# Summing the outputs of 64 experts into the tokens: 0/1 products on TensorE in place of a scatter to memory, with the down product moved inside each step

## What is computed

```python
MOE_EXPERTS = 32; MOE_TOP_K = 2; EXPERT_HIDDEN = 512   # D_MODEL 1024, SEQ 512
...
    gp, gi = lax.top_k(group_prob, 1)          # one of 4 groups
...
    ev, ei = lax.top_k(sel, MOE_TOP_K)         # two of its 8 experts
    gates = gp * jax.nn.softmax(ev, axis=-1)
...
        hid = jax.nn.silu(xblk @ w_gate[e]) * (xblk @ w_up[e])
        return hid @ w_down[e]
...
    yr = yb.reshape(n_rows, d).astype(F32) * row_gate[:, None]
    return jax.ops.segment_sum(yr, row_tok, num_segments=n_tok).astype(x2.dtype)
```

## Time and profile before

| | us |
|---|---|
| median of 3 runs | 1770.22 |
| the profiled execution: its own time | 1770.5 |
| its span, from the first to the last instruction | 1768.7 |
| TensorE busy | 1561.2 |
| VectorE busy | 565.6 |
| ScalarE busy | 323.9 |
| GpSimd busy | 133.4 |

### The profile page before, as it was taken

The page is one execution under the profiler, slowest core; times in us unless marked ns, Lnnn a source line. Parts: engine busy times, 40 slices in busy tenths (PEclk is TensorE's granted clock), DMA queues, the critical chain, the costliest instruction groups (busy, mean ns, idle before and its releaser), DMA issues.

```text
span 1768.7 us, 22309 instructions
## 1 busy us (share of the span) xinstructions
PE 1561.2 (88%) x9199; PEld 1003.0 (57%) x9199; DVE 565.6 (32%) x924; ACT 323.9 (18%) x547; POOL 133.4 (8%) x136
## 2 busy tenths in 40 slices
PE   8999998987788777879999999999997878977776
PEld 6876785543344444437777787878653444544342
DVE  4899743110101101125452444454311101101104
ACT  4225630100000000023221222222010000000002
POOL 0030001111011011000000000000110110111010
PEclk9999999999999999999999999999999999999998
DMA  8521157999999999995122122227599999999996
GB/s 290 191 76 68 60 197 273 401 400 392 398 406 407 399 399 406 397 366 193 60 95 96 48 96 95 84 107 304 214 396 404 409 406 409 402 402 404 400 404 254
DMA packets 117930, 495.60 MB, mean 280 GB/s; under 512 B 14153, under 2 KB 26441, under 8 KB 84928
## 3 DMA queue, kind: packets, MB, share of 16 engines
q1 hardware_dynamic: 104576, 467.69, 67.8%
q0 software_dynamic: 10176, 16.24, 2.8%
q10 hardware_dynamic: 3072, 10.18, 1.5%
HBM read 484.66 MB, written 26.74 MB: 289 GB/s over the span
## 4 chain that ended last, share of the span: by engine, by line
PE 46%; SPq 30%; DMA 14%; DVE 6%; issue 2%; ACT 1%; DVEq 0%; ACTq 0%; POOLq 0%
SPq L771 30%; PE psum L833 9%; PE psum L834 8%; PE psum L835 8%; PE psum L917 6%; PE psum L941 3%; DMA in_pair<-in_expert_w_up 3%; DMA in_uT<-in_expert_w_up 3%; DMA raw<-in_expert_w_up 3%; DMA raw<-in_expert_w_gate 3%; PE psum L1287 2%; DVE xs L1701 2%; PE psum L926 2%; PE psum L908 1%; DMA xs_dram<-xs 1%
## 5 line engine op out<-in xcount | busy, mean ns | idle before, releaser
L917 PE MATMUL psum<-raw,xeT 128*64 128x256 f32 x2048 | 247.2, 388 | 79.9 <-DMA raw<-in_expert_w_gate 41.1
L917 PEld LDWEIGHTS psum<-raw,xeT 128*64 128x64 f32 x2048 | 145.1, 138 | 171.7 <-DMA raw<-in_expert_w_up 51.0
L1987 DVE TENSOR_TENSOR hid<-silu_g,psum 128x256 f32<-128x256 f32 (+1 forms) x64 | 27.5, 430 | 650.4 <-PE psum L917 621.7
L917 PE MATMUL psum<-in_pair,xeT 128*64 128x256 f32 x1280 | 155.7, 390 | 49.3 <-DMA in_pair<-in_expert_w_up 33.8
L647 DVE TENSOR_TENSOR w_lo<-raw,w_hi 128x2048 fp32r<-128x2048 f32 x46 | 105.4, 2291 | 202.2 <-ACT w_hi L641 202.2
L917 PEld LDWEIGHTS psum<-in_pair,xeT 128*64 128x64 f32 x1280 | 90.5, 139 | 108.5 <-DMA in_pair<-in_expert_w_up 47.5
L641 ACT ACTIVATE w_hi<-raw 128x2048 fp32r<-128x2048 f32 x46 | 88.0, 1914 | 339.1 <-PE psum L835 335.0
L1496 ACT ACTIVATE y_e<-psum 64x512 f32<-64x512 f32 (+1 forms) x60 | 35.6, 594 | 597.7 <-PE psum L941 575.8
L833 PE MATMUL psum<-w_hi,uT_hi 128*128 128x512 f32 x352 | 139.1, 395 | 1.6 <-DVE h L2130 1.4
L835 PE MATMUL psum<-w_lo,uT_hi 128*128 128x512 f32 x352 | 137.2, 390 | 0.0
L834 PE MATMUL psum<-w_hi,uT_lo 128*128 128x512 f32 x352 | 137.1, 390 | 0.0
(11 more groups left out here) (245 smaller groups left out, 1935.3 us busy)
## 6 DMA issues: line engine op xcount, KB each, us to landing
raw<-in_expert_w_gate SPq DMA_DIRECT2D x88, 1024.0 KB, 24.2
raw<-in_expert_w_up SPq DMA_DIRECT2D x44, 1024.0 KB, 24.6
free_a<-in_expert_w_down SPq DMA_DIRECT2D x44, 1024.0 KB, 24.9
free_b<-in_expert_w_down SPq DMA_DIRECT2D x44, 1024.0 KB, 24.9
in_pair<-in_expert_w_up SPq DMA_DIRECT2D x42, 1024.0 KB, 24.6
in_uT<-in_expert_w_up SPq DMA_DIRECT2D x42, 1024.0 KB, 24.7
in_pair<-in_expert_w_gate SPq DMA_DIRECT2D x40, 1024.0 KB, 24.2
xs<-in_expert_w_down SPq DMA_DIRECT2D x40, 1024.0 KB, 24.9
```

The costliest lines, as they stand in the source:

```text
L917: mm = nc.tensor.matmul(psum[c * FIRST:(c + 1) * FIRST, bank, 0:HID // 2], x[:, j, 0:FIRST], w[:, j, c * HID // 2:(c + 1) * HID // 2], sta ...
```

## The change

What it does:

- All 32 experts are summed by 0/1 products. Each result is scaled by its gate on the way out of PSUM and split into `y_hi` (ScalarE) and `y_lo` (VectorE), both fp32r. In every second step the two finished experts of the pair before are added to the four tiles of tokens: per tile eight products (two experts, high and low, two halves of 512 columns) into PSUM banks 1 and 7, then VectorE adds both banks to `h` (`add_sum`). The 0/1 matrices are made per tile and pair by VectorE (`tokens_of`). The last three experts (29 to 31) are summed at the end (`last_sums`).
- The scatter, `y_dram` in the usual path, the eight loads back, the eight stores of zeros, `gate_early` and `gate_diag` are gone. They stay only for `over_pass`.
- A step on TensorE becomes: gate, turn `hid` of the last step, turn the next tokens, down of the last step, up. The queue of weights follows this order (`BLOCKS`).
- VectorE works out a gate for each slot of each step (`place_gates`) before step 0.
- Tokens are turned at a width of 64 (before: 96), all eight pieces in one bank.

```diff
-EARLY = 3
+EARLY = 4
...
+BLOCKS = ([("gate", 0), ("up", 0)] +
+          [block for e in range(1, STEPS) for block in (("gate", e), ("down", e - 1), ("up", e))] + [("down", STEPS - 1)])
...
+SUM_BANKS = (1, 7)
+SUMS = [(e, e + 1) for e in range(0, BIG, 2)] + [(BIG,)] + [(e, e + 1) for e in range(BIG + 1, STEPS - 3, 2)]
+SUM_IN_STEP = {steps[-1] + 2: n for n, steps in enumerate(SUMS)}
+LAST = tuple(range(SUMS[-1][-1] + 1, STEPS))
...
+                def sum_tile(e, q):
...
+                    pe.wait_ge(m.token_ok, at + 1)
+                    pe.wait_ge(m.y_lo_ok, past + SUMS[n][-1] + 1)
+                    if at:
+                        pe.wait_ge(m.added, at)
...
+                    for i, of in enumerate(SUMS[n]):
+                        for y in (y_hi, y_lo):
+                            for half in range(2):
+                                r = slice(0, P) if of == BIG else slice(half * FIRST, (half + 1) * FIRST)
+                                src = y[half] if of == BIG else y[of % 2][r]
+                                mm = nc.tensor.matmul(psum[:, SUM_BANKS[half]], to_token[r, at % 2, i], src,
+                                                      start=(i == 0 and y is y_hi), stop=(of == SUMS[n][-1] and y is y_lo))
+                    mm.then_inc(m.summed, 1)
...
                 for e in range(STEPS):
                     if e:
-                        turned(e - 1)
+                        pe.wait_ge(m.silu_ok, past + e)
...
+                    w, ready = weights("gate", e)
+                    product(xeT[:, e % 2], w, 2, ready, m.gate_psum)
+                    if e:
+                        turned(layer, e - 1)
+                    sum_tile(e, 0)
...
+                        transpose_tokens(m, x_e[:, (e + 1) % 2], rows_in_step(e + 1))
+                    sum_tile(e, 1)
                     if e:
-                        down(e - 1)
...
+                        down(layer, e - 1, *weights("down", e - 1))
+                    sum_tile(e, 2)
+                    w, ready = weights("up", e)
+                    product(xeT[:, e % 2], w, 3, ready, m.up_psum)
+                    sum_tile(e, 3)
...
+            def add_sum(layer, n, q):
+
+                dve.wait_ge(main.summed, sum_no(layer, n, q) + 1)
+                for half in range(2):
+                    dst = h[:, q, half * 512:(half + 1) * 512]
+                    ins = V.tensor_tensor(dst, dst, psum[:, SUM_BANKS[half]], ALU.add)
+                ins.then_inc(main.added, 1)
...
+                    n = SUM_IN_STEP.get(e)
+                    if n is not None:
+                        add_sum(layer, n, 0)
+                        tokens_of(layer, n, 2)
+                    if e < STEPS - 1:
+                        copy_tokens(m, past + e + 2, xeT[:, (e + 1) % 2], rows_in_step(e + 1))
+                    if n is not None:
+                        add_sum(layer, n, 1)
+                        tokens_of(layer, n, 3)
+                        add_sum(layer, n, 2)
+                    elif e:
+                        keep_y(layer, e - 1)
...
-            def scatter(m, e, b):
-
-                G.indirect_dma_start(y_dram, bass.IndirectOffsetOnAxis(ap=rows_of(e, 1), axis=0), y_e[0:rows_in_step(e), b], None,
-                                     bounds_check=TOPK * SEQ - 1, oob_is_err=False).then_inc(m.scattered[b], 16)
```

More of the change, by code:

```diff
@@ L1074, in over_pass, with last_sums, some @@
                 pe.wait_ge(over_landed[layer], over_total(layer))
-            def sums(layer):
-                def last_rows(q, i, start=False, stop=True, counted=False):
-                    for n, y in enumerate((last_hi[i][:, :], last_lo[:, i])):
+            def last_sums(layer, last_down, spilled):
+                m, past = main, STEPS * layer
+                slot = [e % 2 for e in LAST[:-1]] + [2]
+                def some(q, i):
+                    for n, y in enumerate((y_hi[slot[i]], y_lo[slot[i]])):
                         for half in range(2):
@@ L1087, in last_rows @@
+                            if i == len(LAST) - 1 and n:
                                 mm.then_inc(bank_full[b], 1)
-                def gated_rows(q, half, first=True):
-                    b, _, _ = banks.at("last", layer, q, half)
-                    c = slice(half * 512, (half + 1) * 512)
-                    pe.wait_ge(rows_in[q], 32 * (layer + 1) + 16)
-                    pe.wait_ge(diag_ok, sum(len(tiles) for tiles in BY_PRODUCT[:layer + 1]) * TOPK)
-                    for k in range(TOPK):
-                        mm = nc.tensor.matmul(psum[:, b], gate_diag[:, BY_PRODUCT[layer].index(q) * TOPK + k], y_back[k][q][:, c],
-                                              start=(first and k == 0), stop=(not first and k == TOPK - 1))
-                    return mm
@@ L1100, in sums, with early @@
-                pe.wait_ge(last_lo_ok, 2 * layer + 1)
-                last_rows(0, 0, True, False)
-                pe.wait_ge(last_lo_ok, 2 * layer + 2)
-                for q in range(TILES if layer else TILES - 1):
-                    by_product = q in BY_PRODUCT[layer]
-                    if by_product:
-                        for half in range(2):
-                            gated_rows(q, half)
-                    if q:
-                        last_rows(q, 0, not by_product, False)
-                    last_rows(q, 1, counted=True)
+                def early(q):
+                    for i in range(len(LAST) - 1):
+                        some(q, i)
@@ new lines, in last_sums @@
+                turned(layer, STEPS - 1)
+                if spilled:
+                    down(layer, STEPS - 1, *last_down)
+                    over_pass(layer)
+                pe.wait_ge(m.last_token_ok, layer + 1)
+                pe.wait_ge(m.added, sum_no(layer, len(SUMS) - 1, TILES - 1) + 1)
+                pe.wait_ge(m.y_lo_ok, past + STEPS - 1)
+                early(0)
+                early(3)
+                if not spilled:
+                    down(layer, STEPS - 1, *last_down)
@@ L1111, in sums @@
+                early(1)
+                pe.wait_ge(m.y_lo_ok, past + STEPS)
+                for q in range(TILES):
+                    if q == 2:
+                        early(2)
+                    some(q, len(LAST) - 1)
                 if not layer:
-                    q = TILES - 1
-                    last_rows(q, 0, True, False)
-                    last_rows(q, 1, stop=False)
                     norm_tile(2, 0)
-                    for half in range(2):
-                        b, _, _ = banks.at("last", layer, q, half)
-                        gated_rows(q, half, False).then_inc(bank_full[b], 1)
```

420 lines of the change are left out of this document (204 added, 216 removed).

## The result

The changed kernel takes 1721.09 us (median of 4 runs, 1718.56 to 1725.76) against 1769.43 us (4 runs, 1768.29 to 1770.52): a ratio of 0.9728, interval 0.9714 to 0.9741. It is 48 us faster; 40 were forecast. The profiled execution is the slowest of the four, 1725.76 us, so trace stands against trace with 44.7 us. In a few runs of several kernels, the one before among them, TensorE's granted clock was 0.96 to 0.97 and the time 2% longer; no comparison or range here holds one of these.

The account below looks back on a forecast made before the run. An expert stage was taken to be bound by weight transfers. -16.8 - 4.9 - 13.9 + 0.5 - 4.6 = -39.7 from 1770.5 gave 1731 us; likeliest case (both sides near 472 us, 55%) 1722 to 1742, range 1710 to 1753.

Parts of the forecast that it names:

- The idle spell: Weight queue near the start of each layer's expert stage: blocks asked for in order of use remove 5 us idle.
- The scatter: Transfers in the expert stages: dropping it saves 0.55 us in each of 29 steps, 16 us a layer (10 to 25).
- Transfers 470.8 and 466.4: First gate product to last up product in layers 0 and 1, in us, if transfers alone set the time.
- TensorE, 472: TensorE's own need per layer from first gate to last up product: 395.5 us plus 76.5 us of sums.
- x: TensorE's cost of one group of sums, taken as 5.1 us; the change is 30x - 197 us, no gain at 6.6.
- The additional 3 and 1.5 us for two equal chains: Expert stages of layers 0 and 1: added because TensorE and transfers at times wait for each other.
- Tails: From U, the end of a layer's last up product: -4.9 us to layer 0's second weight split, -4.6 to the last norm.
- Rival 1: Sums on TensorE cost more, x of 6.8 to 8.2, and the kernel is slower: 1777 to 1819 us; 7%.
- Rival 2: Sums cost somewhat more, x of 5.6 to 6.4, and TensorE binds alone: 1742 to 1765 us; 15%.
- Rival 3: Cheap sums, x of 4.4, and a dear scatter, 0.87 us a step: 1705 us, with half of this 1718; 16%.
- Rival 4: Transfers do not shrink without the scatter; only the gains from idle queue and layer ends come: 1751 us; 5%.
- rival 5: Second pass runs or block order leaves the weight queue as idle as before: within 0.2% or slower; 2%.

Follow-up runs that it names:

- the order alone: The kernel before with only the new order of products on TensorE and of blocks in the weight queue, scatter and loads back kept: 1757.56 us.
- the low part twice: The changed kernel with the products of y_lo in the sums issued twice: 1775.53 us, ratio to the kernel before 1.0032.

## Why the prediction held

The forecast was 1731 us, its likeliest range 1722 to 1742, the whole range 1710 to 1753; 1721.1 lies just below the likeliest case's own range. The mechanism held: two nearly equal bounds took the place of one. Of the 10 us that it is off, 5 are the spread of the changed kernel (its profiled run is 4.7 us above its median), 5 are in the terms. That some terms came out so closely is in part luck, as two of them below show.

- **The idle spell, -5 us a layer.** Right in layer 0 (-5.4 by the order alone), half in layer 1 (-2.6), for a reason that stays open.
- **The scatter, -0.55 us a step.** Right where the transfers alone bind: 0.59. Put back beside the full sums it was worth 11.1 and 9.2 us a layer, where 16 and 10 were forecast. Its share was taken as half of 5.3%; it was 2.1 points, 5.5 engine-us a step and 0.35 us if spread evenly. So the step's forecast was right with too large a share and too even a spread: 0.59 is 1.7 times the even 0.35, near the doubling that half of the engines would give, but no view here shows single engines, and the share of 0.46 at 772 us is a mean that doesn't tell how many were done. The Trainium skill (DMA: Bandwidth & Descriptors, The descriptor swizzle) has partitions 0 to 31 on engines 0 to 7 in a transfer to 128 partitions. A factor of 1.7 does not contradict that, but a scatter of 64 slots is not that transfer, and the -25 us that the rule was taken to give was 17.1.
- **Transfers 470.8 and 466.4.** Measured 470.7 and 468.0.
- **TensorE, 472.** Layer 1, where nothing else bound, took 473.4. This is partly luck, for the parts missed in opposite directions: x was 5.3 against 5.1, a step without sums 11.9 (23.78 / 2) against 12.07, and the clock, for which the sum has no term, cost 2.2 and 4.1 us. At the full clock it is 469.3 to 469.5. The first pair of a tile takes 0.34, the others 0.23 to 0.24, as read from the earlier trace rows. The Trainium skill (TensorEngine Tiling (Array Packing), Key Properties) says that a change of mode drains the engine. The 0.1 us that was charged for it, eight times a group, fits the timeline, where the first pair takes from 377.50 to 377.84 us, 0.34 against 0.23.
- **The additional 3 and 1.5 us for two equal chains.** This was the wrong term. In layer 0 the 472.2 are TensorE's 469.5 at the full clock, 2.2 of clock and 0.5 of waiting for the last half block; the one chain hindered the other by that 0.5 us and no more. In layer 1 it did not at all. The missing term for the clock is what makes 473.4 meet the forecast of 473.5.
- **Tails.** -4.7 for -4.6 and, with the 1.5 us at the next block, -5.6 for -4.9. The landing of the next mixer's weights is not what ScalarE waited for: its split starts at U + 10.3, right behind `y_hi`. But the norm starts at U + 15.3, not 13.7. 1.35 us of this is `last_token`, made by VectorE after `hid` only. From U of layer 0 to S of layer 1 the kernels with the new sums take between 469.6 and 471.3 us, so a term under 2 us there, like this 1.5, is not told from the spread by one profile.
- **place_gates, +0.5.** It cost 1.2, inside its bounds of 0 to 1.3.
- **S of layer 0, -1.9.** Not foreseen; the store of rows, which the first gather waited for before (18.7 us, now 16.6), is a wait that the prediction didn't look at.
- **30x - 197, no gain at x = 6.6.** With the low part twice x is 7.2 and the kernel is 0.3% slower than before. By the measured 1721.1 at 5.3 the line crosses zero at 6.9. Rival 1 was thus the right shape at the wrong price: its x of 6.8 would have ended near no change. Rival 2 began at x = 5.6, above the 5.3. It reached up to 1765 us, so the range to 1753 holds only the lower part of it, although the prediction says that it takes it in. Rival 3 asked for a cheap x and a dear scatter, and had neither. Rival 4 fell with the 17.1 us of the scatter, rival 5 with the full queue from S + 8 us on.

## What to carry to other kernels

When a change moves work from the queue that binds to the engine that waits, work out both sides to the microsecond: the gain ends where they meet, and here they met within 2 us in layer 0 and 6 in layer 1. Afterwards a chain of 85% TensorE does not mean that TensorE alone binds; take work away from it and add the same amount, and if only the adding shows in full, there are two bounds and the next gain needs both. Before you compare two such stages to the microsecond, compare the granted clock in them. A small transfer in a full queue can cost more than its bytes: 0.59 us here against 0.35 by bytes.

## What the runs showed of the hardware

- **The time follows TensorE's clock once TensorE binds.** The changed kernel's ten runs lie between 1718.13 us at a mean granted clock of 0.993 and 1725.76 at 0.986, about 1 us for each 0.001. Before, 37 runs from 0.980 to 0.989 lie between 1767.5 and 1773.6 us without such a trend. In the profiled run the clock fell behind TensorE's waits: after the 1.35 us for `last_token` to 0.50 of 2.4 GHz (1.2 GHz), where the last down took 4.53 us and not 3.65. In windows of 2 us:

```profile
757.00:759.00 2.00, 1.53 (x12) 1.25 (x14) 0.42 (x2) 0.00 (x0) 0.00 (x0) 0.90 0.91 340
759.00:761.00 2.00, 2.00 (x10) 0.78 (x8) 0.00 (x0) 0.00 (x0) 0.00 (x0) 0.50 0.70 261
```

- **The clock differs between executions behind the same wait.** The first gate product of layer 1 comes behind a wait of 2.5 us. In six of ten profiles with the new sums it took 5.24 to 5.36 us, partly at 1.2 GHz, and in four 3.67 us at 2.4 GHz.
- **Packets of 8 KB are a little cheaper than two of 4 KB** in a full queue: 0.325 us against 0.17 each, an estimate from the packets and shares of the weight queue. Making a third of the bytes 8 KB packets shortened a stage by 3.5 and 2.5 us of 470. A 2 MB store beside them took 20.1 us and 17.0 without.
- **A pair of products added to a run of pairs costs 0.235 us,** its distance in the timeline, once the clock is taken off: the second low part, 28 us a layer by that price, cost 27.8 and 28.0 us.
